# A transformer pair in one kernel: two levels of the recurrence per turn, and a projection moved ahead of another

## The reference

```python
u = rmsnorm(h, norm1_w[l]) * (1.0 + sc1) + sh1        # sc1, sh1, ... from silu(c) @ w_ada ("modulation")
proj = u @ w_in[l]
hq, hf, hi, hg, aq, ak, av = jnp.split(proj, offs, axis=-1)
o_hg = hgrn2(hq, hf, hi, hg, lower_bounds[l], hgrn_gnorm_w[l])       # gated linear recurrence, 4 heads of 128
o_da = diff_attention(aq, ak, av, lam, lambda_init, diff_subln_w[l]) # 4 heads, two softmaxes each
mix = jnp.concatenate([o_hg, o_da.astype(o_hg.dtype)], axis=-1) @ w_out[l]
h = h + g1 * mix
```

## Time and profile before

| | |
|---|---|
| time, median of 3 runs (lowest, highest) | 1310.8 us (1310.75, 1312.73) |
| the profiled execution: its span, first to last instruction | 1309.3 us; no other time of it is given |
| PE busy | 1265.3 us, 97% |
| PEld (loading weights into the array) | 962.0 us, 73% |
| VectorE, ScalarE, GpSimd busy | 604.8, 485.9, 65.8 us |
| moved by DMA | 349.36 MB, mean 267 GB/s |
| PE's unread products from 114.53 and 130.20 us | 4.13 and 3.57 us |

### The profile page before, as it was taken

One profiled execution on the slowest core, in us unless ns is written; L12 is line 12 of the kernel. 1 busy time (PEld: TensorE's weight loads), 2 busy tenths in 40 slices (PEclk: granted clock), 3 DMA queues, 4 the chain that ended last, 5 costly groups with the idle time before them and its releaser, 6 DMA issues.

```text
span 1309.3 us, 19242 instructions
## 1 busy us (share of the span) xinstructions
PE 1265.3 (97%) x8338; PEld 962.0 (73%) x8338; DVE 604.8 (46%) x967; ACT 485.9 (37%) x732; POOL 65.8 (5%) x70
## 2 busy tenths in 40 slices
PE   8999999999999999999999999999999998989997
PEld 7887888999998989979999999834444343443432
DVE  4576656444556587485655657532122121212112
ACT  4543555434444634444554545421111111111112
POOL 4021000000001121010110000000000000000000
PEclk9999999999999999999999999999999999999999
DMA  9886336555543534443455558879999999999996
GB/s 353 295 287 242 136 128 239 181 192 184 174 150 126 186 110 156 153 164 126 131 151 180 176 182 335 317 317 419 421 421 420 422 421 420 422 421 420 421 420 251
DMA packets 102869, 349.36 MB, mean 267 GB/s; under 512 B 6178, under 2 KB 9536, under 8 KB 78464
## 3 DMA queue, kind: packets, MB, share of 16 engines
q1 hardware_dynamic: 101200, 345.56, 69.6%
q0 software_dynamic: 1408, 2.50, 0.8%
q10 hardware_dynamic: 176, 0.07, 0.0%
HBM read 347.05 MB, written 1.05 MB: 266 GB/s over the span
## 4 chain that ended last, share of the span: by engine, by line
PE 79%; DMA 8%; DVE 7%; ACT 4%; SPq 1%; issue 1%; DVEq 0%; ACTq 0%
PE bank L551 43%; PE bank L948 13%; PE bank L986 6%; DMA arena<-in_expert_w_up 4%; PE bank L747 2%; DVE WHL L1428 2%; DMA arena<-in_expert_w_gate 2%; DMA weights<-in_expert_w_up 2%; PE bank L472 2%; PE bank L578 2%; SPq L2318 1%; PE bank L508 1%; ACT WHL L1006 1%; PE bank L797 1%; PE bank L518 1%
## 5 line engine op out<-in xcount | busy, mean ns | idle before, releaser
L551 PE MATMUL bank<-XH,WHL 128*128 128x256 f32 x2928 | 541.4, 285 | 7.6 <-DVE WHL L1428 3.7
L551 PEld LDWEIGHTS bank<-XH,WHL 128*128 128x128 f32 x2928 | 462.6, 193 | 12.4 <-DVE WHL L1428 5.5
L551 PE MATMUL bank<-XL,WHL 128*128 128x256 f32 x1464 | 415.5, 284 | 0.0
L1428 DVE TENSOR_TENSOR WHL<-weights,WHL 128x1024 fp32r<-128x1024 f32 x223 | 283.0, 1285 | 214.4 <-ACT WHL L1006 214.0
L1006 ACT ACTIVATE WHL<-weights 128x1024 fp32r<-128x1024 f32 x223 | 232.0, 1054 | 216.0 <-PE bank L551 208.0
L551 PEld LDWEIGHTS bank<-XL,WHL 128*128 128x128 f32 x1464 | 282.8, 193 | 0.1
L948 PE MATMUL bank<-arena 128*64 128x512 f32 x584 | 147.4, 595 | 8.4 <-DMA arena<-in_expert_w_gate 5.7
L948 PEld LDWEIGHTS bank<-arena 128*64 128x64 f32 x584 | 46.0, 137 | 98.4 <-issue 80.2
L551 PE MATMUL bank<-WHL,XH 128*128 128x512 f32 x320 | 102.4, 394 | 4.1 <-DVE WHL L1428 4.1
L2149 DVE SCALAR_TENSOR_TENSOR y_lo<-bank,small,y_hi 128x512 fp32r<-128x512 f32 x32 | 24.0, 751 | 129.0 <-ACT y_hi L1402 128.2
L948 PE MATMUL bank<-weights,arena 128*64 128x512 f32 x320 | 76.1, 595 | 3.6 <-DMA weights<-in_expert_w_gate 2.1
(11 more groups left out here) (356 smaller groups left out, 1349.5 us busy)
## 6 DMA issues: line engine op xcount, KB each, us to landing
weights<-in_w_in SPq DMA_DIRECT2D x58, 1024.0 KB, 5.0
arena<-in_expert_w_gate SPq DMA_DIRECT2D x39, 1024.0 KB, 26.1
arena<-in_expert_w_up SPq DMA_DIRECT2D x34, 1024.0 KB, 26.4
arena<-in_expert_w_down SPq DMA_DIRECT2D x25, 1024.0 KB, 26.1
weights<-in_w_ada SPq DMA_DIRECT2D x22, 1024.0 KB, 7.7
weights<-in_expert_w_down SPq DMA_DIRECT2D x22, 1024.0 KB, 26.4
weights<-in_expert_w_gate SPq DMA_DIRECT2D x20, 1024.0 KB, 26.3
weights<-in_expert_w_up SPq DMA_DIRECT2D x20, 1024.0 KB, 26.2
```

The costliest lines, as they stand in the source:

```text
L551: ins = e.matmul(o, l, r, start=first, skip_group_check=True, stop=g.part == g.parts - 1 and k == g.kc - 1 and n == 2)
L1428: e.tensor_tensor(lo, unit_weights(g, u), hi, ALU.subtract).then_inc(S.w_lo, 1)
```

## The change

Four things change, in all engines' programs alike.

1. `hv` is projected before `av` (and its weights are loaded before the modulation parts 8 and 9).
2. The recurrence's lane is first in each turn, and in turns 0, 1 and 2 it takes a second step (`islice(levels, 3)`) behind the modulation's sums. So levels 0, 1, 2 are in turn 0, levels 3 and 4 in turn 1, 5 and 6 in turn 2, 7 in turn 3, 8 in turn 4; the values product is in turn 5, the sums of squares in turn 6, the spread in turn 7. Before, levels 0 and 1 were in turn 0, then one per turn to turn 7, the values product in turn 8, sums and spread in turn 9.
3. `diff` starts at turn 5, not 4, so that its last two steps (of eight) come behind the end of `wo0`, where before only the last one did.
4. The two groups of unread products inside `diff` (36 and 32 passes on PE) are gone. Other calls of `spin` stay.

```diff
-             Gemm("av", win(6), 0, tok=True), Gemm("hv", win(2), 0, tok=True), Gemm("hg", win(3), 0),
+             Gemm("hv", win(2), 0, tok=True), Gemm("av", win(6), 0, tok=True), Gemm("hg", win(3), 0),
...
-        order = ([..., "ak", "ada6", "ada7", "av",
-                  "ada8", "ada9", "hv", "hg", "wo0", ...
+        order = ([..., "ak", "ada6", "ada7", "hv",
+                  "ada8", "ada9", "av", "hg", "wo0", ...
...
-                        if step == 1:
-                            spin(by["hv"].banks[0], 16)
...
-                        if step == 0:
-                            spin(by["hv"].banks[0], 18)
...
# tensor
-            weave([gemm(n) for n in ("aq", "ak", "av", "hv", "hg", "wo0")],
-                  (0, ada(ada_sum, range(4, 10))),
-                  (-1, gated(HG, [(S.hb, 1), by["hq1"].freed[1]], by["hv"].freed[1])),
-                  (0, ada(ada_turn, range(4, 10))), (4, diff()), (9, gated_spread(HG, S.hg_n)))
+            levels = gated(HG, [(S.hb, 1), by["hq1"].freed[1]], by["hv"].freed[1])
+            weave([gemm(n) for n in ("aq", "ak", "hv", "av", "hg", "wo0")], (-1, levels),
+                  (0, ada(ada_sum, range(4, 10))), (0, islice(levels, 3)), (0, ada(ada_turn, range(4, 10))),
+                  (5, diff()), (7, gated_spread(HG, S.hg_n)))
...
# scalar
-                  (0, ada(range(4, 10))), (-1, gated(HG)), (4, diff()))
+                  (-1, levels), (0, ada(range(4, 10))), (0, islice(levels, 3)), (5, diff()))
...
# vector
-                  (-1, gated(HG, [(S.hb, 1), by["hq1"].freed[1]])), (0, ada(range(4, 10))), (4, diff()))
+                  (-1, levels), (0, islice(levels, 3)), (0, ada(range(4, 10))), (5, diff()))
```

More of the change, by code:

```diff
@@ L2 @@
 from contextlib import ExitStack
+from itertools import islice
 import concourse.bass as bass
@@ L356, in build @@
         ADA = [0, 2, 1] + list(range(3, 12))
-        order = (["ada0", "ada2", "hf0", "hq0", "ada1", "ada3", "hf1", "hq1", "aq", "ada4", "ada5", "ak", "ada6", "ada7", "av",
-                  "ada8", "ada9", "hv", "hg", "wo0", "wo1", "ada10", "ada11", "fg0", "fu0", "fg1"]
+        order = (["ada0", "ada2", "hf0", "hq0", "ada1", "ada3", "hf1", "hq1", "aq", "ada4", "ada5", "ak", "ada6", "ada7", "hv",
+                  "ada8", "ada9", "av", "hg", "wo0", "wo1", "ada10", "ada11", "fg0", "fu0", "fg1"]
                  + [g.name for g in G[by["fu1"].unit0 and G.index(by["fu1"]):]])
@@ L1275, in scalar @@
             run(hq1)
-            weave([gemm("aq", to_features(aq, scale=0.125)), gemm("ak", to_features(ak)), gemm("av", to_tokens(av)),
-                   gemm("hv", to_tokens(hv)), gemm("hg", to_features(hg, func=ACT.Silu, after=[(S.hb, 1)])),
+            levels = gated(HG)
+            weave([gemm("aq", to_features(aq, scale=0.125)), gemm("ak", to_features(ak)), gemm("hv", to_tokens(hv)),
+                   gemm("av", to_tokens(av)), gemm("hg", to_features(hg, func=ACT.Silu, after=[(S.hb, 1)])),
                    out_of_hgrn()],
-                  (0, ada(range(4, 10))), (-1, gated(HG)), (4, diff()))
+                  (-1, levels), (0, ada(range(4, 10))), (0, islice(levels, 3)), (5, diff()))
             for k in range(4, KC):
@@ L1901, in vector @@
             run(hq1)
-            weave([gemm("aq"), gemm("ak"), gemm("av"), gemm("hv"), gemm("hg"), out_of_hgrn()],
-                  (-1, gated(HG, [(S.hb, 1), by["hq1"].freed[1]])), (0, ada(range(4, 10))), (4, diff()))
+            levels = gated(HG, [(S.hb, 1), by["hq1"].freed[1]])
+            weave([gemm("aq"), gemm("ak"), gemm("hv"), gemm("av"), gemm("hg"), out_of_hgrn()],
+                  (-1, levels), (0, islice(levels, 3)), (0, ada(range(4, 10))), (5, diff()))
             w.wait_ge(S.mod, 10)
```

## The result

The changed kernel is slower: 1326.0 us, the median of 4 runs (1324.8 to 1327.2), against 1310.9 for the kernel before, a ratio of 1.0106 with a 95% interval of 1.0092 to 1.0119. Run once more beside the experiments it took 1324.5 (1323.7 to 1326.4) against 1311.7, ratio 1.0097 [1.0080, 1.0113]. The forecast was 1318.3 with a range up to 1321.5: the direction was right, the size was not (7.5 us forecast, 15.1 measured, 12.8 beside the experiments).

What follows compares the result with a forecast made beforehand. PE was taken to bound 65.8 to 191.5 us. Removed products (-7.7) and added waits gave +5.3, the clock +2.2: +7.5 us, span 1309.3 to 1316.8, median 1.5 above, so 1318.3 us; range 1313.0 to 1321.5.

Steps and rivals of the forecast that it cites:

- A: Rival: faster, the early norm pays and nothing waits from turn 6 on; -3.6 us, 1307.2 us; chance 8%.
- D: Rival: PE shifts as forecast, but DMA holds the end; within 0.2%, about 1311 us; chance 11%.
- B: Rival: no fall of the clock; +5.3 us, 1316.1 us; chance 26%.
- C: Rival: clock falls at three places, or a table load lies behind its wait; about +10.5, 1321.3 us; chance 15%.
- turn 0: From 65.80 us, PE waits for VectorE's masked copy, GpSimd's keys and ScalarE's row copy: +3.7 us.
- row copies: Turns 3, 4, 5: no level between sums and turning, so PE waits 0.65 us each for the row copy: +2.0 us.
- turn 9: Behind the ninth half projection, the weights of head 3 come late: +0.6 us.
- before `wo0`: PE waits for `hg`'s late evacuation, then XH and XL: 3.5 us instead of 1.7, +1.8 us.
- before `wo1`: Two late attention steps leave VectorE's products and reciprocal uncovered before the last spread: +1.6 us.
- The clock: Half clock after waits of 2 us and more: 0.5 in turn 0 plus 1.7 before `wo0`, +2.2 us.
- The removed products: Two groups of unread products on PE's chain, 4.13 and 3.57 us, go: -7.7 us.
- The end: The shift at the first product of `wo1` was carried unchanged to the program's end; no separate term.

Runs made afterwards that it cites:

- e1: The changed kernel, unaltered, run once more beside the experiments: 1324.5 us.
- e3: The changed kernel with both groups of unread products put back at the same steps of the attention: 1324.9 us.
- e2: The kernel before with only the two groups of unread products taken out: 1317.7 us, ratio 1.0046.
- f4: The changed kernel with 34 unread products added in five of PE's waits for experts' weights: 1321.35 us.
- f3: The changed kernel with one level per turn, sums ahead of it and spreads in turn 9, as before: 1318.2 us, ratio 1.0044.
- f2: The changed kernel with its three extra levels in turns 1 to 3 instead of 0 to 2: 1326.9 us.
- g3: The kernel before with 34 more unread products in the experts' waits: 1316.0 us, ratio 1.0026.
- g1: The changed kernel with 42 unread products in PE's waits: turn 0, ahead of the recurrence's values, before `wo0` and before `wo1`: 1318.7 us.
- j1: The changed kernel with 34 unread products fitted to PE's waits in turn 0, before the recurrence's values, `wo0` and `wo1`, and in the experts: 1318.4 us.

## Why the prediction was wrong in size

**PE bounds the stretch, and a shift at `wo1` reaches VectorE's last instruction: right.** The 9.2 us at `wo1` were 9.9 at VectorE's last instruction. But `wo1` itself started later than the 198 to 199.5 us forecast, at 201.06 in e1. Rivals A and D are out, and B, because falls did come. C, with three falls on the path, came nearest and was still 3.2 us short of e1, 4.7 of the first measurement.

**The waits: right.** Forecast +13.0 us against -7.7. In e1's trace, which has no early fall, idle time from turn 0 to `wo1` is 15.1 us against 3.15, +12.0. Busy time fell by 2.7 us, which is -7.7 + 3.4 of clock + 1.6; the 1.6 I put down to the restarts behind the new waits, whose first products show longer, but no run isolates it. One by one (forecast / measured, over before): turn 0 3.7 / 3.7; row copies 2.0 / 2.2; values 1.2 / 1.3; head 1's scores 0.6 / 0.6; turn 7 1.5 / 1.2; turn 9 0.6 / 0; before `wo0` 1.8 / 1.5; before `wo1` 1.6 / 1.4. Only turn 9 was not there.

**The clock: the mechanism was right, the term was mis-sized.** The price of a fall, 1.7 us, held. The number didn't: I let only waits of 2 us and more count. In e1 two falls lie on the path before `wo1`, 3.4 us instead of 2.2: the one I placed before `wo0`, and one in `av`, behind waits of 0.7 and 1.3 us, which I had not. A third stands behind `wo1`'s waits of 1.43 and 1.08. The fall in turn 0 cost nothing: with it or without it, the second half of `aq` comes 12.9 us after the turn's start, as it only eats the waits for GpSimd and for the row copy, which e1's timeline of PE shows:

```profile
75.36 2.05 PE L579 MATMUL bank<-arena 128*128 128x128 f32 x16 [1.00 <-POOL arena L2208]
78.09 1.05 PE L519 MATMUL bank<-fold,arena 128*128 128x1 f32 x8 [0.67 <-ACT arena L1078]
```

**The removed products: right as work, wrong as a gain.** "No other product goes, so all the rest is waits" counted -7.7 us, and PE was rid of them. But in the changed kernel they would also have kept the clock in `av`, and their number decides the end: put back (e3), they cost 5.1 us up to `wo1` and nothing in the median. In the old order, as e2 shows, they covered 5.3 us of waits and three falls, and kept 3.3 us off the end.

**The end: the step that failed.** I carried the shift at `wo1` to the end as if nothing behind VectorE's last instruction could change; the term was put at nothing without a reason. PE's closing branch got 3.1 to 3.5 us longer there, and f4 takes 3.1 us of it back with 34 products that stand far from the change. This is the largest single part of the miss; the mis-sized clock is the other. With the clock's 1.2 us more and about 1.2 behind `wo1`, where e1's trace has three falls and that of the kernel before two, this is e1's difference: 7.5 + 1.2 + 0.5 + 1.2 + 3.1 = 13.5, measured 13.9 with 0.3 at the start (0.5 is what the waits and restarts together have over my waits). The first profiled execution had the early fall in addition, 2.8 us.

**By parts of the change**, from before through e2 and f3 to e1, by medians: without the groups +6.0 (3.3 of it the end); `hv` first and the attention later +0.5, which is no more than "before" moved between the groups; two levels per turn, with the early spread, +6.2. f4 says that 3.1 of the whole 12.8 are the end.

## What to carry to other kernels

Before taking out work that nobody reads, lay the waits beside it: it may be holding a clock, and it is worth its time where it is cut to the length of the wait. Several short waits close together (here 0.7, 1.3 and 0.7 us) can have a fall of the clock behind them as a long one does, and not every time: f2 has the same three waits and no fall there. And compare the time from the last instruction to the end of the span before explaining a difference of a few microseconds by the work: here a quarter of the loss was there, in one branch of PE's queue, and in g3 most of it.

## What the hardware showed unexpectedly

- The gap from VectorE's last instruction to the span's end is 2.1 us or 5.2 to 5.7 us, by the number of PE's instructions, not their place: PE's closing branch takes 0.48 us or 3.55 to 3.97 us, and in the long case a packet of the instruction queue arrives about 1 us into it. That the branch waits for instructions to be fetched is an inference: what is shown is that 34 products in the experts' stage switch it.
- A fall of the granted clock from 1.00 to 0.50 (2.4 to 1.2 GHz) costs 1.7 us and followed idle time of PE: a single wait of 1.4 us (at 418 us), or a group of waits of 0.7 to 1.3 us (in `av`). With products in the waits it stayed at 1.00 in g1 and j1. The same wait has it in one execution and not in another: the one of 2.4 us in turn 0 in the first trace, not in e1's; the pair of 1.43 and 1.08 us before `wo1` in e1's, not in e3's. No run here separates what decides it.
- ScalarE's table load ran ahead of a wait of 1.78 us and cost nothing.
